# Attention on two heads at once: scores in row halves, values in column groups, outputs transposed

## What is computed

```python
def fox_attend(q, k, v, fq, fk, qpos):
    logits = jnp.einsum('bqhd,bkhd->bhqk', q, k).astype(jnp.float32) * HD_A ** -0.5
    logits = logits + fq.transpose(0, 2, 1)[..., None] - fk.transpose(0, 2, 1)[:, :, None, :]
    causal = jnp.arange(k.shape[1])[None, :] <= qpos[:, None]
    logits = jnp.where(causal, logits, NEG_INF)
    p = jax.nn.softmax(logits, axis=-1).astype(v.dtype)
    return jnp.einsum('bhqk,bkhd->bqhd', p, v)
...
def merge(x, branches, w_gate_l, b_gate_l, w_branch_l, w_out_l):
    gates = jax.nn.sigmoid((x @ w_gate_l).reshape(*lead, N_BRANCH, D_MODEL) + b_gate_l)
    o = jnp.stack(branches, axis=-2)
    br = jnp.einsum('...nw,nwd->...nd', o, w_branch_l)
    return (gates * br).sum(-2) @ w_out_l
```

## Time and profile before

| | |
|---|---|
| median of 3 runs | 1622.12 us (1619.0 to 1623.43) |
| the profiled execution | 1617.91 us |
| its span | 1616.0 us, mean granted TensorE clock 0.948 |
| PE / PEld busy | 1467.4 / 1128.8 us |
| DVE / ACT / POOL busy | 779.4 / 441.7 / 308.9 us |

### The profile page before, as it was taken

One profiled execution on the slowest core, in us unless ns is written; L12 is line 12 of the kernel. 1 busy time (PEld: TensorE's weight loads), 2 busy tenths in 40 slices (PEclk: granted clock), 3 DMA queues, 4 the chain that ended last, 5 costly groups with the idle time before them and its releaser, 6 DMA issues.

```text
span 1616.0 us, 20546 instructions
## 1 busy us (share of the span) xinstructions
PE 1467.4 (91%) x7704; PEld 1128.8 (70%) x7704; DVE 779.4 (48%) x1412; ACT 441.7 (27%) x737; POOL 308.9 (19%) x222
## 2 busy tenths in 40 slices
PE   7999889899998988999999999999965989999980
PEld 3465477644455778999999999968853656666650
DVE  1266544422025553223333444445575666777746
ACT  1211134301104321111111111121222455666646
POOL 1148900035222023000000000000031621222210
PEclk9879999999999998999999999999977999999995
DMA  7337610145431002222232242332274999887655
GB/s 213 108 122 249 225 64 1 40 126 197 156 121 40 1 33 85 75 75 85 75 101 75 101 153 78 100 117 67 79 296 172 379 318 307 303 297 249 205 181 214
DMA packets 75199, 237.74 MB, mean 147 GB/s; under 512 B 17029, under 2 KB 27476, under 8 KB 61422
## 3 DMA queue, kind: packets, MB, share of 16 engines
q1 hardware_dynamic: 48630, 160.73, 27.5%
q0 software_dynamic: 17792, 59.20, 12.5%
q10 hardware_dynamic: 8704, 16.84, 3.0%
HBM read 213.49 MB, written 65.74 MB: 173 GB/s over the span
## 4 chain that ended last, share of the span: by engine, by line
PE 74%; DVE 7%; DMA 6%; POOL 4%; issue 4%; ACT 4%; SPq 0%; POOLq 0%; DVEq 0%; ACTq 0%
PE ps L470 14%; PE ps L472 14%; PE ps L471 14%; PE ps L1225 10%; PE ps L1206 5%; DMA tmp_yd<-b,b 4%; PE ps L601 4%; PE ps L1318 3%; PE ps L1343 3%; POOL b L1960 3%; POOL tmp_xs L1058 1%; PE ps L1396 1%; DVE b L1792 1%; DMA b<-in_cache_k,b 1%; PE ps L1240 1%
## 5 line engine op out<-in xcount | busy, mean ns | idle before, releaser
L470 PE MATMUL ps<-b,b 128*128 128x344 f32 (+1 forms) x1360 | 472.9, 348 | 14.9 <-DVE b L762 3.8
L471 PE MATMUL ps<-b,b 128*128 128x344 f32 (+1 forms) x1360 | 468.2, 344 | 0.0
L472 PE MATMUL ps<-b,b 128*128 128x344 f32 (+1 forms) x1360 | 467.8, 344 | 0.0
L470 PEld LDWEIGHTS ps<-b,b 128*128 128x128 f32 x1360 | 257.1, 189 | 35.0 <-issue 12.3
L472 PEld LDWEIGHTS ps<-b,b 128*128 128x128 f32 x1360 | 257.1, 189 | 19.4 <-issue 0.9
L471 PEld LDWEIGHTS ps<-b,b 128*128 128x128 f32 x1360 | 257.1, 189 | 17.0 <-issue 0.8
L1225 PE MATMUL ps<-b,b 128*128 128x512 f32 (+1 forms) x640 | 257.1, 559 | 0.0
L1225 PEld LDWEIGHTS ps<-b,b 128*128 128x128 f32 x640 | 122.0, 194 | 120.7 <-issue 116.1
L989 DVE TENSOR_TENSOR b<-b,b 128x2048 fp32r<-128x2048 f32 x64 | 146.3, 2290 | 46.0 <-ACT b L686 43.2
L1206 PE MATMUL ps<-b,b 128*128 128x128 f32 (+1 forms) x814 | 127.6, 286 | 44.5 <-DMA b<-tmp_xs 18.5
L1058 POOL DMA_INDIRECT tmp_xs<-b,b x36 | 46.3, 1285 | 622.7 <-issue 565.0
(11 more groups left out here) (266 smaller groups left out, 1324.9 us busy)
## 6 DMA issues: line engine op xcount, KB each, us to landing
b<-in_w SPq DMA_DIRECT2D x96, 1024.0 KB
b<-in_w_merge SPq DMA_DIRECT2D x32, 640.5 KB, 4.3
tmp_xs<-b ACTq DMA_DIRECT2D x32, 514.0 KB, 3.8
b<-tmp_xs SPq DMA_DIRECT2D x32, 514.0 KB
b<-in_w_in SPq DMA_DIRECT2D x8, 1024.0 KB, 8.4
b<-in_xT SPq DMA_DIRECT2D x4, 1024.0 KB, 12.5
b<-in_w_out SPq DMA_DIRECT2D x4, 1024.0 KB, 8.9
b<-in_x SPq DMA_DIRECT2D x8, 512.0 KB, 3.7
```

The costliest lines, as they stand in the source:

```text
L470: mm(out, hi, mhi, start=start, stop=False)
L471: mm(out, hi, mlo, start=False, stop=False)
L472: return mm(out, lo, mhi, start=False, stop=stop)
```

## The change

Both heads of a pair are worked on together. `UNITS` = (query tile, head pair), 16 for a branch; two units (tiles 2j and 2j + 1) are a pair in `PAIRS`, 8 for a branch.
- Scores: head hh of the pair uses rows 64 hh to 64 hh + 63 of q and k as they are, and banks of its own; the zeroed copies of q, their memsets, and one of the two `qk_evict` steps go away. A unit has its scores in two banks, or one for each head where qt < 4.
- Values: stationary v (64 columns of a head), moving the transposed weights of both query tiles (256 columns), the two heads to partitions 0 to 63 and 64 to 127 of bank 6. The output is transposed as it comes, so `out_transposes` and its copies go away. The inverse sums are spread by matmuls of `arec` with the identity to bank 7, and DVE multiplies straight to `oT` (`norm`, now 8 times).
- PE's order is scores(u + 1), values of the last pair at every second unit, transposes(u, 0), transposes(u, 1). DVE's is the inverse sums, shifted(u + 1) of both heads, norm, blocks(u) of both heads.
- `p_sb` becomes four buffers, `p_T` two of 256 columns a block.
- In A the projections of qkc for the sample rows and for tile 0 move ahead of the last values (`tail_a`). In C the last norm moves behind the first `split_weights`.
- The eight `split_x` move from DVE to POOL, between `load_values_c` 3 and 6; the splits of the outputs of branches B to D move from POOL to DVE, one at the start of each merge round; the clearing of `zeros` moves from DVE to POOL.
- The decode values of C come at pairs 1, 2, 4 and 5, two at a time.

Removed lines of the functions printed above are left out.

```diff
+        halves = [at(PSB, [P, SEQ]), at(PSB + 4096, [P, SEQ])]
+        pbuf = [halves + [at(OT + 2 * (TOKB // 4) + o, [P, SEQ]) for o in (0, 4096)],
+                halves + [at(NAT, [P, SEQ]), at(TMP, [P, SEQ])]]
+        pT_even, pT_odd = at(RING + TOKB, [P, NT, 2 * P]), at(PD, [P, NT, 2 * P])
+        def pT_of(br, hh):
+            return pT_even if hh == 0 else vp[:, :, W:2 * W] if br else pT_odd
...
+        PAIRS = [(j, hp) for j in range(NT // 2) for hp in range(H // 2)]
+        UNITS = [(2 * j + a_, hp) for j, hp in PAIRS for a_ in range(2)]
+        WIDE = [sum(qt >= 4 for qt, _ in UNITS[:u]) for u in range(2 * len(PAIRS) + 1)]
...
-        VALUES_C = {3 + 2 * b: b for b in range(NB)}
-        HEADS_C = 22
+        VALUES_C = {1: (0, 1), 2: (2, 3), 4: (4, 5), 5: (6, 7)}
+        HEADS_C = 6
...
             for n in range(4):
                 if n:
                     pe.wait_ge(S("os"), N("os", n))
+                else:
+                    pe.wait_ge(S("x2"), N("x2", 2 * KD))
...
             split_weights(0, 16, 1)
+            last_norm()
             dve.wait_ge(S("out_vc"), 16)
-            link(dve.tensor_copy(oH[:, 0], oT[:, 0]))
-            link(dve.tensor_tensor(oL[:, 0], oT[:, 0], oH[:, 0].bitcast(F32), ALU.subtract))
-            dve.sem_inc(S("so"), 1)
-            link(dve.memset(zeros[:], 0.0))
-            dve.sem_inc(S("zeroed"), 1)
+            def split_out(n):
+                link(dve.tensor_copy(oH[:, n], oT[:, n]))
+                return dve.tensor_tensor(oL[:, n], oT[:, n], oH[:, n].bitcast(F32), ALU.subtract)
+            split_out(0).then_inc(S("so"), 1)
+            dve.wait_ge(S("oD"), 1)
             for n in range(4):
+                if n < 3:
+                    split_out(n + 1).then_inc(S("os"), 1)
                 with dve.Fori(0, KD // 2 - (n == 3)) as i:
                     for u in range(2):
                         merge_weight(i, n, u, False)
...
+            def attention(br, bias_ready, v_of, side, tail):
+                pt_used = [32 * br, 16 * br]
+                def scores(u):
+                    qt, hp = UNITS[u]
                     L = P * (qt + 1)
...
+                    if u:
+                        pe.wait_ge(S("sc_free"), 32 * br + (2 * u if qt >= 4 else 2 * (u - 1)))
                     for c in range(0, L, 512):
                         e = min(L, c + 512)
...
+                        for hh in range(2):
+                            lo = 64 * hh
+                            bank = 2 * hh + (c // 512 if qt >= 4 else u % 2)
+                            m = mm(ps[:, bank, 0:e - c], qT[lo:lo + 64, hp, qt * P:(qt + 1) * P], kT[lo:lo + 64, hp, c:e],
+                                   start=True, stop=br == 1 or e < L)
+                            if br == 1 and e == L:
+                                m.then_inc(S("sc"), 1)
+                    if br == 0:
+                        for hh in range(2):
+                            bank = 2 * hh + ((L - 1) // 512 if qt >= 4 else u % 2)
+                            w = (L - P) % 512
+                            mm(ps[:, bank, w:w + P], ident[:], causal[:], start=False, stop=True).then_inc(S("sc"), 1)
+                def transposes(u, hh):
+                    qt, hp = UNITS[u]
+                    n = 2 * u + hh
                     pe.wait_ge(S("ex"), 32 * br + n + 1)
                     for c in range(1 + (qt >= 4)):
...
+                        pe.wait_ge(S(f"pt_free{c}"), 32 * br + n if c == 0 else 16 * br + 2 * WIDE[u] + hh)
                         for k in range(4 * c, min(qt + 1, 4 * c + 4)):
...
+                            m = tr(ps[:, 4 + c, (k % 4) * P:(k % 4 + 1) * P], pbuf[br][n % 4][:, k * P:(k + 1) * P])
                         m.then_inc(S(f"pt{c}"), 1)
...
+                def values(i):
+                    j, hp = PAIRS[i]
+                    pe.wait_ge(S("rec"), 8 * br + i + 1)
+                    pe.wait_ge(S("on"), 8 * br + i)
+                    for a_ in range(2):
+                        for hh in range(2):
+                            col = 4 * (i % 2) + 2 * a_ + hh
+                            mm(ps[64 * hh:64 * hh + 64, 7, a_ * P:(a_ + 1) * P], arec[:, col:col + 1].to_broadcast([P, 64]), ident[:],
+                               start=True, stop=True)
+                    side(i)
+                    pe.wait_ge(S("pt_free0"), 32 * br + 4 * (i + 1))
+                    if j >= 2:
+                        pe.wait_ge(S("pt_free1"), 16 * br + 2 * WIDE[2 * i + 2])
+                    for k in range(2 * j + 2):
+                        lo = 0 if k <= 2 * j else P
+                        for hh in range(2):
+                            m = mm(ps[64 * hh:64 * hh + 64, 6, lo:2 * P], v_of(k, 2 * hp + hh), pT_of(br, hh)[:, k, lo:2 * P],
+                                   start=(k == 0), stop=(k == 2 * j + 1))
                     m.then_inc(S("pv"), 1)
...
                 bias_ready()
                 scores(0)
...
+                for u in range(16):
+                    if u < 15:
+                        scores(u + 1)
+                    if u % 2 == 0 and u:
+                        values(u // 2 - 1)
+                    transposes(u, 0)
+                    transposes(u, 1)
+                tail()
+                values(7)
             def bias_a():
                 pe.wait_ge(S("fb"), 8)
                 pe.wait_ge(S("evicted"), 27)
                 pe.wait_ge(S("qkT_qka"), 8)
...
+            def tail_a():
+                pe.wait_ge(S("sc_free"), 32)
+                project("qkc", NT)
+                project("qkc", 0)
...
@@ -1478,15 +1489,13 @@
                 pe.wait_ge(S("oDn"), 6)
                 pe.wait_ge(S("so"), 1)
-            def side_c(n):
-                if n in VALUES_C:
-                    values_of_c(VALUES_C[n], n)
-                if n == HEADS_C:
-                    heads_out(1, 6 + n % 2)
-            attention(1, bias_c, lambda k, h: vp[:, k, h * 64:h * 64 + 64], side_c)
-            pe.wait_ge(S("on"), 64)
-            pe.wait_ge(S("pt_free0"), OUT_DONE[1])
+            def side_c(i):
+                for n, b in enumerate(VALUES_C.get(i, ())):
+                    values_of_c(b, 7 - n)
+                if i == HEADS_C:
+                    heads_out(1, 7)
+            attention(1, bias_c, lambda k, h: vp[:, k, h * 64:h * 64 + 64], side_c, lambda: None)
...
@@ -1563,37 +1572,31 @@
                 act.copy(vo[:, b, :], ps[:, 2 + b % 2, 0:W]).then_inc(S("vo"), 1)
             def attention(br):
...
+                def weights(u, hh):
+                    qt, hp = UNITS[u]
+                    n = 2 * u + hh
+                    p_ = pbuf[br][n % 4][:, 0:P * (qt + 1)]
                     act.wait_ge(S("sc_free"), 32 * br + n + 1)
...
+                    act.activation(p_, p_, ACT.Exp, scale=-1.0, bias=am[:, n % 8:n % 8 + 1],
+                                   accum_out=asum[:, n % 8:n % 8 + 1]).then_inc(S("ex"), 1)
+                def blocks(u, hh):
+                    qt, hp = UNITS[u]
+                    nb = min(4, qt + 1)
+                    act.wait_ge(S("pt0"), 32 * br + 2 * u + hh + 1)
+                    if u >= 2 and u % 2 == 0:
+                        act.wait_ge(S("pv"), 8 * br + u // 2)
+                    act.copy(pT_of(br, hh)[:, 0:nb, u % 2 * P:u % 2 * P + P],
+                             ps[:, 4, 0:nb * P].rearrange("p (k r) -> p k r", r=P)).then_inc(S("pt_free0"), 1)
+                weights(0, 0)
+                weights(0, 1)
+                for u in range(16):
+                    for hh in range(2):
+                        blocks(u, hh)
+                        if u < 15:
+                            weights(u + 1, hh)
             def values_ready(i):
...
                     if i == 1 and chunk == "qka":
                         dve.wait_ge(S("out_vb"), 16)
-                        link(dve.memset(qT[64:P], 0.0))
                     src = ps[:, 4 + t % 2, :].rearrange("p (f r) -> p f r", f=4)
-                    for h in range(2):
-                        dve.tensor_scalar(q_of(br, h)[64 * h:64 * h + 64, :, t * P:(t + 1) * P], src[64 * h:64 * h + 64, 0:2, :],
-                                          SCALE, None, ALU.mult)
+                    dve.tensor_scalar(qT[:, :, t * P:(t + 1) * P], src[:, 0:2, :], SCALE, None, ALU.mult)
                     link(dve.tensor_copy(kT[:, :, t * P:(t + 1) * P], src[:, 2:4, :]))
                     dve.sem_inc(S(f"qkT_{chunk}"), 1)
...
@@ -1783,61 +1781,77 @@
             def attention(br, bias_of, side):
...
+                def shifted(u, hh):
+                    qt, hp = UNITS[u]
                     L = P * (qt + 1)
+                    n = 2 * u + hh
                     dve.wait_ge(S("sc"), 32 * br + n + 1)
...
+                    if n >= 4:
+                        dve.wait_ge(S("pt0" if UNITS[u - 2][0] < 4 else "pt1"),
+                                    32 * br + n - 3 if UNITS[u - 2][0] < 4 else 16 * br + 2 * WIDE[u - 2] + hh + 1)
```

(87 more changed lines are left out.)

169 lines of the change are left out of this document (21 added, 148 removed), and 2 rows, old and new, of the table GOES_ON.

## The result

The changed kernel takes 1566.78 us (median of 4 runs, 1561.53 to 1567.51) against 1620.56 for the kernel before on the same chip (1613.44 to 1623.43): ratio 0.9666, 95% interval 0.9645 to 0.9686. I had forecast 1563.0, with 1545 to 1600 as range. The profiled execution took 1567.51, its span is 1565.7, the mean granted clock 0.949.

The account below looks back on a forecast made before the run. PE, busy for 91% of the span, was taken as the bound. Savings of 21.8 (A), 2.2 (around A), 23.8 (C) and 11.5 (C to the merge) sum to 59.3, so 1622.1 becomes 1563 us, range 1545 to 1600.

Parts of the forecast that it names:

- A, 79.8 forecast: Attention of branch A: 63.5 of PE slots plus 16.3 idle, 79.8 us against 101.6, saving 21.8.
- The row halves: Scores of two heads side by side in row halves: 1.8 of a possible 2, 17.2 us a branch against 31.0.
- Rival (a): Row halves of the scores don't overlap: scores back at 31.0, 13.8 more a branch, 1591 in all; chance 0.10.
- my bound of 0.14 for one: PE's tiling mode changes in attention: one costs between 0 and 0.14 us, taken as 0.1.
- Values whole: Attention's value matmuls: column packing of two heads taken as complete, 15.5 us a branch against 31.1.
- Rival (d): Neither packing works in attention: 27.6 more for rows and 31 for values, 1622, no change; chance 0.03.
- Hand-offs: Attention: second-head transposes wait 11.4 us for ACT's copies; waits for DVE's bank-5 copies add 2.4 in A, 4.2 in C.
- Rival (b): Every second-head transpose waits 0.6 more because DVE's copies queue behind shifted() and norm(): 19 more, 1582; chance 0.12.
- Around A: From A's last values to the next projection but one: 18.1 us before, 15.9 after including the tail, saving 2.2.
- C, 82.2 forecast: Attention of branch C: 63.3 of PE slots plus 18.9 idle, 82.2 us against 106.0, saving 23.8.
- Rival (c): TensorE's clock falls in both attention stages, sign a clock not over 0.95: 96 more than forecast, 1659; chance 0.07.
- C to the merge: From C's last values into the merge: PE's loss falls from 15.3 to 3.8 us, saving 11.5.

Follow-up runs that it names:

- the two runs on it: Both against the changed kernel: scores contracting over all 128 rows again, 1584.24 us; in A's wide tiles the mask between the two score chunks, 1567.41 us.
- full rows: Changed kernel with scores contracting over all 128 rows again, using q copies with the other head's rows at zero: 1584.24 us, ratio 0.9785.
- by head: Changed kernel with value matmuls reordered, all key blocks of the first head and then all of the second: 1582.68 us in one run.
- Two banks: Changed kernel with the second head's transposes of query tiles 0 to 3 sent to the unused bank 5: 1557.71 us, ratio 0.961.
- the moves alone: Kernel before with x split on POOL, output splits on DVE between merge rounds and zeroing on POOL, attention as before: 1605.01 us, ratio 0.9911.
- their undoing: Changed kernel with the outputs of B, C and D split on POOL behind C again, while DVE splits A's output: 1574.19 us, ratio 0.97.
- its undoing: Changed kernel with the eight splits of x back on DVE, one behind each of units 1 to 8 of attention C: 1569.11 us, ratio 0.9681.

## Why the prediction was right, point by point

- **A, 79.8 forecast, 81.3 measured.** Two misses cancel in the level. The slots were 63.5 in my sum and are 70.0: scores 18.7 (17.2), values 16.4 (15.5), broadcasts 3.9 (3.5), mask 9.6 (6.9), transposes 21.4 (15.6), with my 4.8 for changes of mode now inside these. The idle time was 16.3 and is 11.3; a part of this is bookkeeping, as the end of the last transpose before a wait counts as slot in the trace and as idle in my sum. The kernel before has the same miss: PE is busy 91.7 of its 101.6 us, where my sum had 86.3 of slots. So the differences were right one by one, and not by luck: the slots fell by 21.7 (22.8 forecast) and the idle time grew by 1.4 (1.0 forecast).
- **The row halves.** My 1.8 of 2 was right for the longest tile (3.43 / 1.91) and wrong as a kind of number: the streams halve, and there is a fixed 0.21 for each group with some 0.1 on either side, 6.5 a branch, where my 1.7 and my share of the changes (32 x 0.1) made 4.9. For one key block the row halves gain nothing (0.42 against 0.44). Rival (a) is out. The Trainium skill (TensorEngine Tiling (Array Packing), Key Properties) has a change of tiling mode drain the engine; the two runs on it agree that a change costs something, 0.3 to 0.4 us for entering and leaving together, where my bound of 0.14 for one allows 0.28. The estimate from the Trainium skill (TensorE: Matmul & The Clock Gate, Measured speedup vs the span model), 1.54 times and 20.1 a branch, was as far off as mine on the other side: A's scores took 18.7, against 31.1 on full rows 1.66 times.
- **Values whole.** Right, as long as the heads stand in turn: by head, A and C lose 10.8 and 10.2. Rival (d) is out with (a).
- **Hand-offs.** ACT's copy between the heads: 11.4 forecast, 9.7 in A and 8.9 in C. DVE's copies: 2.4 and 4.2 forecast, 1.2 and 1.7 measured. Two banks take half of the wait for ACT's copy away (4.8 left in A, 4.1 in C), so the cause holds. Rival (b) is out.
- **Around A, 15.9 forecast, 16.1 measured** (8.9 in the tail, 7.2 behind it), so 2.0 saved for 2.2. Put back, the projections cost 4.3, more than I credited: in the tail they also run at the full clock, while behind the chain's wait the next one runs in part at the lower clock. That the idle stayed was in the forecast; that it could be covered by the order alone was not.
- **C, 82.2 forecast, 87.0 measured.** The step that failed: I priced C wholly at full clock. The lower clock costs 5.1 of its 87 us; without them it is 81.9. The same two misses as in A cancel below that: at full clock 69.7 of slots for 63.3, and 12.2 idle for 18.9. The 32 small matmuls (4.6, not 3.5) and the sixth values behind them (5.7 in place of 3.3) are the larger part, C's start the other. The kernel before lost 3.2 in C, so the mechanism was to be seen there. Rival (c) is out in A (1.00); in C the clock is 0.94, just below the 0.95 that I had named as its sign, and it cost 5.1 us, not the 44 of the rival.
- **C to the merge, 11.5 forecast, 13.0 measured.** PE loses 0.9, not 3.8: it waits 0.50, and the clock doesn't fall. The contention of DVE and POOL is shown from both sides, by the moves alone (9.4) and by their undoing (7.5). The waiting for whole instructions is in the earlier trace rows too: POOL's subtract ends at 606.14, 2.31 behind it is 608.45, and DVE's subtract ends at 608.31. x on POOL is part of C's gain (2.5 us by its undoing, 3.2 by the moves alone, without the clock), which my sum had within C's idle; its last split ends at 491.3, before C is half done, as forecast.
- **The sum.** By stage 22.3 + 0.2 + 19.0 + 13.0 = 54.5, against 59.3 forecast; the gap is C's 4.8, and what A and its surroundings lack (1.7) the merge gives back (1.5). That last one is luck. The medians differ by 53.8. Of them scores in row halves make some 16 (9.2 + 6.9; 19.5 with C at the same clock), values in turn at least 21 (10.8 + 10.2, as by head they still overlap at each switch), the moves some 13. Each was taken back by itself, so this is no exact division.

## What to carry to other kernels

Price packing as a fixed cost for each group and a stream that halves, and put work that packs into few long groups; matmuls for different column halves must alternate in the queue. Before work is moved ahead as filler, look at the next wait: the projection of tile 0 was worth more over DVE's chain behind A (8.6 us, 2.5 of them clock) than in the tail. And let DVE and POOL do long elementwise steps at different times where PE waits for one of them, and price the overlap, where there is one, as waiting for the other's whole instruction.

## What the runs showed of the hardware that I had not expected

- Two heads in row halves: 0.21 + 0.213 us a key block, against 0.43 on full rows. One more entry costs 0.21 in its own slot and 0.3 in all.
- 32 matmuls that stream 2 columns each are followed by a stretch at the lower of the two clocks, in both places tried, though PE is busy without a gap: 0.69 over 11 us in the change, which is 6.8 us at half clock, and 0.69 over 5.5 us at C's end, which is 3.4. Without them the stretch ran at 1.00.
- C's first 13 us ran at 0.68, 0.69, 0.74, 0.87 or 1.00 in kernels whose code there is the same. What decides that is open.
- A DVE cast or subtract that begins while POOL casts or subtracts waits for POOL's instruction to end: a cast with one input took 3.56 us beside a POOL subtract, and 0.82 alone, and it ended 0.68 behind POOL's. A DVE step with one operand in PSUM took 0.51 in the middle of a POOL subtract.
- The experts' stage took 364.5 to 373.4 us in kernels with the same code, so a difference below 9 us in a single trace's span says nothing until the stages are compared. Most of the spread goes with one wait for a DMA, 8.6 to 16.6 us of ACT's time.
